# Routing of each token tile inside the output projection, with counters carried from tile to tile, in place of one routing pass after it

## What is computed

```python
scores = jax.nn.sigmoid(h.astype(jnp.float32) @ w_router.astype(jnp.float32))
biased = (scores + b_router.astype(jnp.float32)).reshape(N, N_GROUPS, EXPERTS_PER_GROUP)
gscore = lax.top_k(biased, 2)[0].sum(-1)
gsel = lax.top_k(gscore, 1)[1]
cand = jnp.take_along_axis(biased, gsel[:, :, None], axis=1)[:, 0]
loc = lax.top_k(cand, TOP_K)[1]
eidx = gsel * EXPERTS_PER_GROUP + loc
wts = wts / wts.sum(-1, keepdims=True)
...
buf = jnp.zeros((P, D), h.dtype).at[dest].set(h[tok_s])
def expert_block(args):
    xb, e = args
    return (jax.nn.silu(xb @ w1[e]) * (xb @ w3[e])) @ w2[e]
```

## Time and profile before

| | us |
|---|---|
| runs | 2759.95, 2760.31, 2760.97 |
| median | 2760.31 |
| profiled execution | 2761.06 |
| its span (first to last instruction) | 2759.5 |
| TensorE busy | 2497.7 (91%) |
| VectorE busy | 1823.7 (66%) |
| ScalarE busy | 1292.1 (47%) |
| GpSimd busy | 276.2 (10%) |

### The profile page before, as it was taken

The page is one execution under the profiler, slowest core; times in us unless marked ns, Lnnn a source line. Parts: engine busy times, 40 slices in busy tenths (PEclk is TensorE's granted clock), DMA queues, the critical chain, the costliest instruction groups (busy, mean ns, idle before and its releaser), DMA issues.

```text
span 2759.5 us, 29480 instructions
## 1 busy us (share of the span) xinstructions
PE 2497.7 (91%) x10787; PEld 1783.1 (65%) x10787; DVE 1823.7 (66%) x1678; ACT 1292.1 (47%) x1230; POOL 276.2 (10%) x330
## 2 busy tenths in 40 slices
PE   6999889957999999999389988998994999999993
PEld 3555445536888888888178765554453888888883
DVE  2999943226888888888457422554115888888885
ACT  2000121006777777776232323454013777777773
POOL 0535403110000000000100020000001000000001
PEclk9999999968999999999699999999996999999997
DMA  8010437078999999997811321103428999999993
GB/s 322 31 61 31 174 139 273 23 307 308 381 388 388 383 391 385 385 386 296 336 63 62 109 106 58 65 27 125 162 85 318 376 385 387 381 392 385 384 382 115
DMA packets 150402, 672.83 MB, mean 244 GB/s; under 512 B 24714, under 2 KB 34186, under 8 KB 93890
## 3 DMA queue, kind: packets, MB, share of 16 engines
q1 hardware_dynamic: 127698, 592.72, 55.7%
q0 software_dynamic: 20208, 74.98, 7.2%
q10 hardware_dynamic: 2432, 4.26, 0.4%
HBM read 612.58 MB, written 59.33 MB: 243 GB/s over the span
## 4 chain that ended last, share of the span: by engine, by line
PE 86%; DMA 5%; DVE 3%; ACT 2%; POOL 1%; issue 1%; SPq 1%; POOLq 0%; DVEq 0%; ACTq 0%
PE ps L779 83%; ACT arena L1232 2%; PE ps L943 1%; PE ps L949 1%; DMA xs_d<-arena 1%; DMA buf_d<-arena,slots 1%; DMA chunk<-in_w_ada_dram 1%; DMA arena<-buf_d,slots 1%; POOL buf_d L714 1%; PE ps L867 1%; DMA arena<-in_w_out_c_dram 0%; SPq L385 0%; DMA arena<-buf_d 0%; DMA buf_d<-arena 0%; POOL arena L660 0%
## 5 line engine op out<-in xcount | busy, mean ns | idle before, releaser
L1771 DVE TENSOR_TENSOR wl<-wx,wh 128x2048 fp32r<-128x2048 f32 x432 | 969.3, 2287 | 65.7 <-ACT wh L1232 65.6
L1232 ACT ACTIVATE wh<-wx 128x2048 fp32r<-128x2048 f32 x432 | 819.4, 1915 | 155.8 <-PE ps L779 147.0
L779 PE MATMUL ps<-arena 128*128 128x512 f32 (+5 forms) x2436 | 819.3, 510 | 33.5 <-ACT arena L1232 19.7
L779 PE MATMUL ps<-wh,xT 128*128 128x512 f32 x2304 | 736.3, 396 | 4.9 <-DVE xT L1788 4.9
L779 PEld LDWEIGHTS ps<-arena 128*128 128x128 f32 (+1 forms) x2436 | 432.5, 192 | 406.2 <-issue 362.7
L779 PEld LDWEIGHTS ps<-wh,xT 128*128 128x128 f32 x2304 | 435.0, 189 | 105.8 <-DVE xT L1788 5.7
L779 PE MATMUL ps<-wl,xT 128*128 128x512 f32 x1152 | 455.1, 395 | 0.0
L1232 ACT ACTIVATE arena<-ps 128x512 f32<-128x512 f32 (+4 forms) x281 | 171.6, 640 | 512.8 <-PE ps L779 444.7
L779 PE MATMUL ps<-wh,gT 128*128 128x512 f32 x1152 | 378.2, 399 | 0.0
L1232 ACT ACTIVATE arena<-arena 128x1024 f32<-128x1024 f32 (+3 forms) x53 | 50.0, 948 | 449.0 <-DVE arena L1627 257.4
L779 PEld LDWEIGHTS ps<-wl,xT 128*128 128x128 f32 x1152 | 217.6, 189 | 47.1
(11 more groups left out here) (230 smaller groups left out, 1927.5 us busy)
## 6 DMA issues: line engine op xcount, KB each, us to landing
wx<-in_w_dram SPq DMA_DIRECT2D x432, 1024.0 KB, 7.8
arena<-in_w_ada_dram SPq DMA_DIRECT2D x40, 1024.0 KB, 10.8
arena<-buf_d POOLq DMA_DIRECT2D x38, 512.0 KB, 9.9
buf_d<-arena POOLq DMA_DIRECT2D x36, 512.0 KB, 7.0
craw<-in_w_in_c_dram SPq DMA_DIRECT2D x8, 2048.0 KB, 8.2
buf_d<-arena POOLq DMA_DIRECT2D x1, 14848.0 KB, 41.5
arena<-in_w_in_ab_dram SPq DMA_DIRECT2D x8, 1024.0 KB, 12.6
arena<-in_w_out_ab_dram SPq DMA_DIRECT2D x4, 2048.0 KB, 8.2
```

Source lines behind the costliest of these rows:

```text
L779: return pe.matmul(bank_ap, lhsT, rhs, start=first, stop=last)
L1232: return act.activation(out_, in_, f, **kw)
L1771: v.tensor_tensor(wl[:, g], wx[:, g], whs[g % NH].bitcast(F32), ALU.subtract).then_inc(m["low"], 1)
```

## The change

Each tile is routed as soon as its logits are there. PE's table `BETWEEN` puts transposes, route, rank matmuls and gate weights at steps of k within the next tiles' projections. ACT takes a sigmoid per tile and loads the square root's function again after it. DVE's one pass is replaced by `mask(t)` and `slot(t)`, which carry a count per expert from tile to tile. An expert whose count passes 128 gets a new block at that point, numbered in order of occurrence. POOL scatters a tile once its slots are there. SP loads item 12 earlier, and items 13, 14 and 15 ahead of expert 0's weights. The buffer is cleared from a tile of 512 columns in place of 1024, with twice the rows.

```diff
+                    if n == 1 and i == NT - 1:
+                        sp.wait_ge(y_mm, NT)
+                        item_load(13)
+                        sp.wait_ge(ge_mm, len(ROUNDS))
+                        item_load(14)
+                        sp.wait_ge(u_in[I_SEM[12]], arrived(12))
+                        item_load(15)
                     if n in (1, 2, 3):
                         sp.wait_ge(x_new, j + 1 - NT)
                         sp.dma_start(xs_d[n][t * P:(t + 1) * P, :], CH[n]["xt"][s]).then_inc(xt_st[s], 16)
...
+                    if n == 1 and i == 2:
+                        sp.wait_ge(h_rdy, NT + 2)
+                        item_load(12)
...
     def scatter(l):
-        pool.wait_ge(sl_rdy, l + 1)
-        tl = tiles_of(1 + 2 * l)
-        for k in range(2):
-            for t, j in tl:
+        for t, j in tiles_of(1 + 2 * l):
+            pool.wait_ge(sl_rdy, routed(1 + 2 * l, t) + l)
+            for k in range(2):
...
-            pool.dma_start(buf_v[:, :, :], bc(zt, 1, NBUF)).then_inc(s_fill, 16)
+            pool.dma_start(buf_v.rearrange("p b (i d) -> p (b i) d", i=2), bc(zt, 1, 2 * NBUF)).then_inc(s_fill, 16)
...
+            def positions(n, t):
+                pe.wait_ge(mk_rdy, routed(n, t))
+                b = route_bank(n, t)
+                mm(ps[:, b, 256:256 + NX], cst[:, C_TRI:C_TRI + P], r_m[:, t, :], True, True)
+                mm(ps[:, b, 256 + NX:256 + 2 * NX], ones[:], r_m[:, t, :], True, True).then_inc(pos_rdy, 1)
...
+                for k in range(kn):
+                    between(n, t, k)
...
             def projected_chain(n, acts, w, kn):
+                for t, j in tiles_of(n):
+                    project(n, t, j, acts, w, kn)
+                to_channels(n, t, j)
+                route(n, t, j)
...
+                    if n in (1, 3):
+                        turned(n, t, j)
+                        act.wait_ge(lg_rdy, routed(n, t))
+                        go(r_sc[:, t, :], ps[:, route_bank(n, t), t * NX:(t + 1) * NX], ACT.Sigmoid).then_inc(sc_rdy, 1)
+                        if t < NT - 1:
+                            go(warm[:, 1:2], ones[:, 0:1], ACT.Sqrt)
...
                     normed(t, j)
+                    if nn in (1, 3):
+                        mask(nn, t)
+                        slot(nn, t)
...
+            def slot(n, t):
+                b = route_bank(n, t)
+                v.wait_ge(pos_rdy, routed(n, t))
+                v.tensor_tensor(r_pos, ps[:, b, 256:256 + NX], r_cnt, ALU.add)
+                link(v.tensor_tensor(r_cnt, ps[:, b, 256 + NX:256 + 2 * NX], r_cnt, ALU.add))
+                v.tensor_scalar(r_in, r_pos, float(P), None, ALU.is_ge)
+                link(v.tensor_scalar(r_new, r_cnt, float(P), None, ALU.is_gt))
+                link(v.tensor_tensor_scan(r_cum, ones[:, 0:NX], r_new, 0.0, ALU.mult, ALU.add))
+                link(v.tensor_scalar(r_nid, r_cum, r_x1, None, ALU.add))
...
+                v.tensor_copy(slots[:, :, t], r_sk).then_inc(sl_rdy, 1)
...
+                link(v.scalar_tensor_tensor(r_cnt, r_new, -float(P), r_cnt, ALU.mult, ALU.add))
+                if t == NT - 1:
+                    link(v.tensor_copy(r_tb[0:1, 31:32], r_x1[0:1, :]))
+                    v.tensor_copy(table[:], r_tb[0:1, :]).then_inc(sl_rdy, 1)
...
+BETWEEN = {
+    1: {(1, 5): [("turn", 0)], (1, 7): [("route", 0)], (2, 3): [("positions", 0)],
+        (2, 10): [("turn", 1)], (2, 13): [("route", 1)], (2, 15): [("weights", 0)], (3, 2): [("positions", 1)],
+        (3, 8): [("weights", 1)], (3, 10): [("turn", 2)], (3, 12): [("route", 2)], (3, 15): [("positions", 2)],
+        (4, 3): [("weights", 2)], (4, 7): [("turn", 3)], (4, 9): [("route", 3)], (4, 13): [("positions", 3)],
+        (5, 2): [("weights", 3)], (5, 5): [("turn", 4)], (5, 8): [("route", 4)], (5, 12): [("positions", 4)]},
+    3: {(CT + i, k): [(what, i - 1)] for i in (1, 2, 3) for k, what in ((5, "turn"), (8, "route"), (12, "positions"))}}
```

More of the change, by code:

```diff
@@ L537, in _ @@
             chain(1)
[L538 to L543, removed]
             expert_weights(0, 0, None, range(PAIRS))
-            sp.wait_ge(u_mm, 13)
-            item_load(15)
             sp.wait_ge(h_rdy, 2 * NT)
@@ L888, in project @@
                 begun = n == 1 and t < 2
-                for i, k in enumerate(range(KD if begun else kn)):
+                kn = KD if begun else kn
+                for k in range(kn):
+                    between(n, t, k)
                     if n == 1 and t in (0, CT) and k < KD:
@@ L892, in project, with between @@
                     for q in range(2):
-                        ins = mm(ps[:, b0 + q, :], acts(k, t), w[q][:, k, :], i == 0 and not begun,
-                                 k == (KD if begun else kn) - 1)
+                        ins = mm(ps[:, b0 + q, :], acts(k, t), w[q][:, k, :], k == 0 and not begun, k == kn - 1)
                 ins.then_inc(y_mm, 1)
+            def between(n, t, k):
+                for what, i in BETWEEN[n].get((t, k), ()):
+                    if what == "turn":
+                        to_channels(n, *tiles_of(n)[i])
+                    if what == "route":
+                        route(n, *tiles_of(n)[i])
+                    if what == "positions":
+                        positions(n, tiles_of(n)[i][0])
+                    if what == "weights":
+                        gate_weights(i)
             def gate_weights(r):
@@ L1073, in _ @@
                 mods(n)
-            pe.wait_ge(ge_rdy, 1)
-            positions(0)
+            positions(1, NT - 1)
             for n in range(14, 16):
                 mods(n)
+            pe.wait_ge(ge_rdy, 1)
             pe.wait_ge(u_ev, 4)
@@ L1221, in _ @@
             mods(36)
[L1222 removed]
+            positions(3, NT - 1)
             for n in range(37, 40):
@@ new lines, in rank @@
+            def rank(dst, a, groups):
+                x1, x2 = (r[:, 0:groups * 16].rearrange("p (g i j) -> p g i j", i=4, j=4) for r in (r_big, r_big2))
+                a = a.rearrange("p (g e) -> p g e", e=4)
+                v.tensor_tensor(x1, bc(a, 2, 4), bc(a, 3, 4), ALU.is_gt)
+                link(v.tensor_tensor(x2, bc(a, 2, 4), bc(a, 3, 4), ALU.is_equal))
+                link(v.tensor_tensor(x2, x2, bc(cst[:, C_TIE:C_TIE + 16].rearrange("p (i j) -> p i j", j=4), 1, groups), ALU.mult))
+                link(v.tensor_tensor(x1, x1, x2, ALU.add))
+                link(v.tensor_reduce(dst.rearrange("p (g e) -> p g e", e=4), x1, AX.X, ALU.add))
@@ new lines, in router_start, with mask @@
+            def router_start():
+                e_row = cst[:, C_E:C_E + NX]
+                v.memset(r_cnt, 0.0)
+                v.memset(r_x1, float(NX))
+                v.memset(r_tb[0:1, NX:32], 0.0)
+                v.tensor_copy(r_tb[0:1, 0:NX], e_row[0:1, :])
+                link(v.tensor_scalar(r_blk, e_row, 1.0, None, ALU.add))
+            def mask(n, t):
+                sc = r_sc[:, t, :]
+                v.wait_ge(sc_rdy, routed(n, t))
+                link(v.tensor_tensor(r_bi, sc, brow[:], ALU.add))
+                rank(r_t, r_bi, 4)
+                link(v.tensor_scalar(r_t, r_t, 2.0, None, ALU.is_lt))
+                link(v.tensor_tensor(r_f, r_bi, r_t, ALU.mult))
+                link(v.tensor_reduce(r_gs, r_f.rearrange("p (g e) -> p g e", e=4), AX.X, ALU.add))
+                rank(r_gr, r_gs, 1)
+                link(v.tensor_scalar(r_gr, r_gr, 1.0, None, ALU.is_lt))
+                v.tensor_tensor(r_m[:, t, :].rearrange("p (g e) -> p g e", e=4), r_t.rearrange("p (g e) -> p g e", e=4),
+                                bc(r_gr, 2, 4), ALU.mult).then_inc(mk_rdy, 1)
+                v.wait_ge(mk_rdy, routed(n, t))
+                v.tensor_scalar(r_nm, r_m[:, t, :], -BIG, BIG, ALU.mult, ALU.add)
+                link(v.tensor_tensor(r_w, sc, r_m[:, t, :], ALU.mult))
+                link(v.tensor_reduce(r_sw, r_w, AX.X, ALU.add))
+                link(v.reciprocal(r_sw, r_sw))
+                link(v.tensor_scalar(r_w, r_w, r_sw, None, ALU.mult))
@@ L1834, in _ @@
             chain(1)
-            router(0)
             experts(0)
@@ L1998, in _ @@
             chain(3)
-            router(1)
             experts(1)
@@ L2011, in lg_before, with routed, route_bank, table_set @@
     return t if n == 1 else NT + t - CT
+def routed(n, t):
+    return lg_before(n, t) + 1
+def route_bank(n, t):
+    return 3 if n == 1 and t == 0 else 6
+def table_set(l):
+    return NT + 1 + l * (NT - CT + 1)
 def y_before(n, t):
```

157 lines of the change are left out of this document (49 added, 108 removed).

## The result

| | before | changed |
|---|---|---|
| median of the runs, us | 2760.2 | 2736.75 |
| lowest and highest | 2759.95, 2760.97 | 2733.56, 2738.19 |
| profiled execution | 2761.06 | 2737.4 |
| its span | 2759.5 | 2735.8 |

The ratio is 0.9913, 95% interval 0.9896 to 0.993: 23.5 us faster where 30 were forecast. The runs of the changed kernel lie 4.6 us apart, those before 1.0.

The account below looks back on a forecast made before the run. PE holds 86% of the chain; the gaps behind the last projections, 74.3 and 61.5 us, were the target. Later projection ends against shorter routing and fewer scatters gave 19.2 + 11.0 = 30.2 us off 2760.3: 2730, range 2714 to 2743.

Parts of the forecast that it names:

- the forecast case: Both layers: the summed terms hold, 19.2 us saved in layer 1 and 11.0 in layer 2, giving 2730; chance 0.55.
- the backlog rival: Behind the projections: last scatter and block 0 come through only when SP's queue is empty, 2740; chance 0.18.
- The last projection ends later.: Projections: post-processing moved in ahead of the last projection's end adds 9.2 us in layer 1, 5.7 in layer 2.
- I take the 6.7 back: Layer 1's projection, 433 to 566: spreading the pieces wins back all 6.7 us lost to a clock averaging 0.95.
- PE waits inside the projections.: Layer 1: PE waits 3.0 us before tile 1's transposes and 1.1 in tile 4; layer 2 waits nowhere.
- the clock's 2.0: Layer 1's projection: a PE wait of 3 us may cost clock, priced at 2.0 us.
- From the last projection to the slots.: Behind the last projection: slots ready 22.1 us later in layer 1 and 20.8 in layer 2, saving only 3 each.
- 12.5 from the first start.: Last two scatters: 4.5 us before data flow, 7.5 alternating with weight packets, 0.5 for the end.
- 10, if the backlog is over: Last two scatters: lower bound of 10 us from first start to landing, with 5.5 us of data movement.
- I take 6.2: Block 0's load after the scatters: 6.2 us, from 3.7 less its own 1.3, plus 3.8 shared.
- The larger-gain rival: Both layers: PE neither waits nor slows and the queue is short, 15 us more gain, 2715; chance 0.19.
- The slower rival: Projections: PE waits for DVE in every tile, 4.6 us in each of 10 tiles, 2776; chance 0.04.

Follow-up runs that it names:

- the late scatters: Changed kernel, but GpSimd waits for the whole table before any scatter: 2777.3 us; with 9 of expert 0's 12 weight pieces also held back, 2747.25.
- the hold: Changed kernel, but SyncE issues 3 of expert 0's 12 weight pieces and the other 9 only after block 0's tokens have landed: 2714.7 us.
- run 15: Not a run's label but part of "run 15 times": the kernel before the change, unchanged, measured 15 times, 2758.5 to 2764.5 us.

## Why the prediction was right, and where it was wrong

The range held the time, and by its signs the forecast case came true: two scatters left, landed ahead of the end of the weights. By the number alone it could not be told: 2736.75 is 6.7 above this case's 2730 and 3.3 below the backlog rival's 2740. Some of the agreement is luck, as said at the steps. Its working, step by step:

- **"The last projection ends later."** The work moved in was sized well: in layer 2, which has nothing but this term, the projection grew by 5.6 us (121.65 for 116.03), forecast 5.7. In layer 1 "I take the 6.7 back" failed: the clock gave away 6.7 us after and 6.9 before. About 3 of the 6.7 came back where the pieces were spread (440 to 566); against them stand 2.9 at the start of the projection, which differ between profiles and which the sum had at nothing. Even there, full clock was not reached. Of two bounds I took the one that needed a reason, and had none but that the pieces were spread.
- **"PE waits inside the projections."** The wait before tile 1's transposes is there, 2.0 us of 3.0 forecast, and 0.7 before tile 0's, which was not forecast; the 1.1 of tile 4 and the clock's 2.0 did not show. In all 2.7 for 6.1. By what was measured, 566.1 + 9.2 - 0.2 + 2.7 = 577.8, against 578.4. The two errors, 6.5 too little and 3.4 too much, leave the forecast 574.7 too early by 3.1 of the 3.7 us; 0.6 stay open. That they offset each other is luck. The pair of profiles is also not typical: over three profiles with the order before (566.1, 565.8, 569.2) and six with the changed order (576.0 to 580.5) the last projection ends 11.0 later on average, forecast 8.6.
- **"From the last projection to the slots."** 21.8 and 21.1 us, forecast 22.1 and 20.8. The lag of POOL was 0.27 in both layers, not 0.9.
- **"12.5 from the first start."** 12.7 and 11.2. The sum was right for layer 1, the reading of its first part was not. I read the 4.5 us before data flow as the indirect DMA's own; with the other queue idle the whole scatter, start to landing, takes 5.0. Its own bound, "10, if the backlog is over", was therefore wrong by half. All the rest, 7.7 us in layer 1, is what lies in the other queue.
- **Block 0's load, "I take 6.2".** 8.1 and 7.9, and 3.8 when alone: mis-sized by 1.9 and 1.7. In layer 1 expert 0's weights still share with all of it: queue 1's packets are of 8 KB until 620 (35 packets, 0.29 MB in 619 to 620). The load's first packet moves at 617, 3.6 us after its start, and its data take 4.5; the forecast had 2.4 and 3.8, and the weights through by 618.
- **The sum.** Layer 1: 3.7 - 0.3 - 0.6 + 0.2 + 1.9 = 4.9 less than forecast, measured 14.4 for 19.2. Layer 2: 10.4 of its own for 11.0. The last 1.3 us were lost between the layers, where nothing was changed; the number of blocks is the same (432 weight loads in both profiles). The small edits, taken as 0, had no run of their own; PE waits at no other place of the two projections.
- **The backlog rival** said that the last scatter would land with the end of the weights. It did not: in layer 1 it landed at 613.1, and queue 1 moved 8 KB packets for 7 us more. But the late scatters show sharing at its full size, and the hold shows that it was the largest term open: 22 us. The larger-gain rival had 9 of them, 2.5 on each scatter and 2 on each load; its 2715 was reached only with the hold.
- **The slower rival,** PE waiting in every tile, needed 3 us per tile; the profile has 2.7 in all before the last. A mask took 3.3 us (592.21 to 595.51) and a slot up to its end 2.8, as summed.

The row of 978 against 979 packets was used for more than it says. Counts over some microseconds come out equal for single alternation and for equal groups in turn. What can be said from rows: behind a full queue the first scatter packet moves some 4 us after the start, with the queue idle 1.4. The difference, 2.6 us at 422 GB/s, is by estimate 1.1 MB or 134 packets of 8 KB, 8 or 9 for each of the 16 engines. The Trainium skill, DMA: Bandwidth & Descriptors, section Queues, rings and completion order, has an engine finish a whole packet of about 9 to 17 descriptors before it changes rings; that agrees with this delay, at its lower end, and the prediction argued against it too quickly. No run shows the groups themselves.

## What to carry to other kernels

Moving work ahead of a late event can gain nothing if other transfers are issued from that event: routing within the projection with late scatters lost 15 us with the weights in the way and nothing with them held back, and only the early scatters made it pay. When a small transfer on the critical path meets a large prefetch, compute when the prefetch is really wanted, and issue ahead of the small one only what will be through when it starts: here holding back 7 of 12 MB gave as much again as the whole change, 2713.8 us for 2736.75. And where a stall's length is read from a stage in which two queues are full, don't take any part of it for a fixed cost before a run has shown it with the other queue empty.

## What the runs showed of the hardware

- Two indirect scatters of 128 rows of 4 KB take 5.0 us from the first start to landing beside an idle queue, 12.7 beside a full one; a contiguous load of 512 KB 3.8 and 8.1. The first scatter packet moves 1.4 us and 4 us after the start.
- Two full queues share by packets, not by bytes: 188 and 188 packets in 5 us, 1.39 MB on the queue whose packets are mostly of 8 KB and 0.70 on that of 4 KB (605 to 610).
- In a row of 8 the fourth scatter's start is busy 1.9 to 2.8 us on GpSimd and not 0.95, in all five profiles with such a row; in a row of 12 the third takes 2.5 in three of five, also with no weights about. Two or six at a time never showed it.
- The changed kernels' times scatter more than the first measurement of the kernel before suggests; that one, run 15 times, also spread over 6 us (2758.5 to 2764.5). The granted clock in 404 to 440 was 1.00, 0.95 and 0.91 in three profiles whose instructions there are the same. Differences under 3 us between two medians say little here.
